# Attention's output projection on high and low parts, in a kernel of many sublayers

## The chip, the cores and the metric

The kernel runs on one core of one Trainium2 chip. The metric is the device time of one execution, in microseconds (us). The engines are named as in the profile: PE is TensorE (matmul), PEld its weight loads, ACT ScalarE, DVE VectorE, POOL GpSimd, SP SyncE. P is 128 partitions, T is 256 tokens, KT is 8 (1024 channels in tiles of 128).

## What is computed

A network of four blocks (each FFN, mixer, FFN, with modulated norms), followed by a second kind of block. The mixers are rwkv, mamba, attention, rwkv. The change is in the attention mixer: 16 query heads of 64, 4 key and value heads, a window of 128.

```
def swa_sink_attention(h, w_qkv, q_norm, k_norm, sinks, w_o):
    ...
    q, k, v = jnp.split(h @ w_qkv, [Hq * Dh, (Hq + Hk) * Dh], axis=-1)
    q = rms_norm(q...); k = rms_norm(k...)
    ...
        s = jnp.einsum('bqkgd,bskd->bkgqs', qb, kbb).astype(f32) * scale
        s = jnp.where(mb, s, NEG_INF)
        m = jnp.maximum(jnp.max(s, axis=-1, keepdims=True), sink)
        p = jnp.exp(s - m)
        denom = jnp.sum(p, axis=-1, keepdims=True) + jnp.exp(sink - m)
        return jnp.einsum('bkgqs,bskd->bqkgd', (p / denom).astype(vbb.dtype), vbb)
    ...
    return o @ w_o

x = x + gate[:, 1, None] * swa_sink_attention(adaln(x, ...), ...)
```

Each sublayer's shift, scale and gate come from `mod = silu(c) @ ada_w + ada_b`, a product of one vector with a large matrix that depends on no activation.

## The kernel before

Every engine has its own program, written out in order; semaphores join them. Weights stream from memory through SP into a ring of three slots of 24 blocks of 128x128 (L476, `weights`); a slot comes free when PE has taken the first block of the next (`Products.take`).

**Matmuls come in two kinds.** A plain one reads fp32 operands; it is recorded as two matmul records. One "on parts" replaces it by three matmuls on fp32r operands (`PAIRS`): weights high by values high, high by low, low by high. The high part is a copy by ACT (`Parts.high`, L1176, 128x1024 for eight blocks), the low part is the difference, taken by DVE (`Parts.low`, L1182). `w_part` is a ring of three such units. The queries and keys of attention are projected on parts (`parts.product`, 12 units); v, the scores, the transposes, the attended values and the output projection are plain.

**The loop over heads** in `sw_products` (PE), `sw_act` (ACT) and `sw_vector` (DVE) is a software pipeline of 19 steps n. In step n, PE makes `scores(n)`, `turns(n-2)` (transposes of the probabilities), half of an output projection tile (`outputs((n-5)//2, half)`, four of the eight output blocks that belong to the pair of heads t, L323) and `values(n-3)`. The projections accumulate in four PSUM banks that stay open for the entire loop. ACT makes the exponentials of head n, evicts the turned probabilities (`turned`), and in even steps evicts the values of a pair of heads (`out(t)`, L2952). DVE makes `largest(n)` (scale, mask and row maxima, L2992 to L2997) and `divided(n-1)` (L3002 to L3005).

**The modulation sums** fill DVE's gaps. `ada_sum` (L507) adds one chunk of 128x1536 of the modulation matrix, 16 chunks for each sublayer, here for the sublayer after next. The chunks come through POOL's queue into two buffers: `ada_stream` (L491) waits until chunk i has been summed, then issues chunk i+2 (768 KB). In attention, chunks 0 to 5 are summed between the projections, 6 to 12 in the odd steps 3 to 15 of the loop, and 13 to 15 behind it. Then DVE splits the first two weight units of the following FFN (`unit_low`, L885) and adds the mixer's output to x (`residual`, L845, eight tiles). ACT squares each new x tile, PE sums the squares (L323, 32 records with an output of 128x4), one small PE product spreads the reciprocal root, and the FFN starts (L928).

The lines at the heart of it:

```
    for n in range(17):
        if n < 16:
            largest(n)
        if n:
            divided(n - 1)
        ...
        elif n >= 3 and n % 2:
            ada_sum(k, dve, u + 2, len(SW_ADA) + (n - 3) // 2)
    for i in range(len(SW_ADA) + 7, ADA_STEPS):
        ada_sum(k, dve, u + 2, i)
```

## Time and profile before

| | us |
|---|---|
| median of 3 runs | 3070.55 (3070.54 to 3078.23) |
| the profiled execution, its own time | 3065.47 |
| its span | 3063.5 |
| PE busy | 2957.7 (97%) |
| DVE busy | 2368.5 (77%) |
| ACT busy | 1395.4 (46%) |
| mean granted TensorE clock | 0.982 |

The attention mixer's products start at 1565 us of the span, its loop over heads at 1612, and the FFN behind it at 1692. In the timeline views, each row is a start, a length, the engine, the line, what is written and read, a count of records, and in square brackets how long the engine was idle before it and what released it. Records of one engine overlap a little, so the step from one start to the next is the cost in a full queue, and the length is a little more.

### The profile page before, as it was taken

How to read it: one execution, taken by the hardware profiler on the slowest of the kernel's cores; microseconds unless marked ns; L12 is line 12 of the kernel's file. 1: busy time of each engine (PE TensorE's matmuls, PEld its weight loads, DVE VectorE, ACT ScalarE, POOL GpSimd, SP SyncE). 2: the span in 40 equal slices, each digit the busy share in tenths (PEclk: the TensorE clock that was granted, in tenths of full speed). 3: DMA queues.
4: the chain of work that ended last, by engine and by line, in shares of the span. 5: the costliest groups of instructions: out<-in, count | busy, mean ns of one | idle time of the engine just before them, and what ended most of it. 6: DMA issues, size and time to landing. Idle time of an engine off the chain costs nothing.

```text
span 3063.5 us, 50589 instructions
## 1 busy us (share of the span) xinstructions
PE 2957.7 (97%) x20226; PEld 2597.7 (85%) x20226; DVE 2368.5 (77%) x3515; ACT 1395.4 (46%) x2214; POOL 97.3 (3%) x187
## 2 busy tenths in 40 slices
PE   7999999999999999999999999999999999999998
PEld 6886788888888888888886888887788888989887
DVE  6988877998878857888867888887855866665685
ACT  4534023545545744545444554544123544465453
POOL 0000000000000000000000000000000000000000
PEclk9999999999999999999999999999999999999899
DMA  8783335686666227575764666672302553444453
GB/s 351 254 310 146 137 116 206 245 301 232 242 231 258 111 104 268 227 288 226 259 247 151 244 251 262 233 272 83 121 19 104 188 190 130 168 151 148 162 187 136
DMA packets 69674, 609.50 MB, mean 199 GB/s; under 512 B 7728, under 2 KB 7888, under 8 KB 31824
## 3 DMA queue, kind: packets, MB, share of 16 engines
q1 hardware_dynamic: 42768, 459.41, 40.3%
q0 software_dynamic: 26352, 144.85, 12.7%
q8 instruction: 161, 2.64, 0.3%
q10 hardware_dynamic: 336, 2.13, 0.2%
q14 instruction: 57, 0.47, 0.0%
HBM read 604.26 MB, written 2.10 MB: 198 GB/s over the span
## 4 chain that ended last, share of the span: by engine, by line
PE 84%; DVE 10%; ACT 3%; DMA 2%; issue 1%; SPq 0%; DVEq 0%; POOLq 0%; ACTq 0%
PE psum L325 25%; PE psum L928 23%; PE psum L932 12%; PE psum L949 10%; PE psum L956 6%; PE psum L323 4%; PE psum L953 1%; DVE arena L814 1%; PE psum L1726 1%; DVE ada_sum L507 1%; DMA weights<-in_weights 1%; DMA ada_in<-in_ada_w 1%; DVE arena L2366 1%; DVE unit_low L885 1%; DVE wkv_base L2102 1%
## 5 line engine op out<-in xcount | busy, mean ns | idle before, releaser
L879 ACT ACTIVATE unit_high<-weights 128x1024 fp32r<-128x1024 f32 x594 | 630.5, 1063 | 681.8 <-PE psum L932 389.5
L885 DVE TENSOR_TENSOR unit_low<-weights,unit_high 128x1024 fp32r<-128x1024 f32 x594 | 725.7, 1223 | 158.4 <-ACT unit_high L879 157.5
L928 PE MATMUL psum<-h_part,unit_high 128*128 128x512 f32 x3168 | 817.2, 395 | 21.2 <-DVE h_part L801 15.1
L928 PEld LDWEIGHTS psum<-h_part,unit_high 128*128 128x128 f32 x3168 | 574.2, 190 | 129.9 <-issue 17.4
L932 PEld LDWEIGHTS psum<-h_part,unit_low 128*128 128x128 f32 x3168 | 443.1, 191 | 29.5
L932 PE MATMUL psum<-h_part,unit_low 128*128 128x256 f32 x3168 | 464.7, 283 | 0.0
L325 PE MATMUL psum<-in_part,w_part 128*128 128x256 f32 x2784 | 358.6, 289 | 7.6 <-issue 3.2
L325 PEld LDWEIGHTS psum<-in_part,w_part 128*128 128x128 f32 x2784 | 344.9, 194 | 24.3 <-ACT arena L1214 11.3
L949 PE MATMUL psum<-hidden,unit_high 128*128 128x512 f32 x1386 | 350.0, 394 | 0.0
L1054 DVE TENSOR_REDUCE arena<-psum 128x256 f32<-128x512 f32 x396 | 272.9, 689 | 55.4 <-PE psum L932 44.5
L507 DVE SCALAR_TENSOR_TENSOR ada_sum<-ada_in,c_act,ada_sum 128x1536 f32<-128x1536 f32 x154 | 278.9, 1813 | 35.0 <-DMA ada_in<-in_ada_w 35.0
L949 PEld LDWEIGHTS psum<-hidden,unit_high 128*128 128x128 f32 x1386 | 249.9, 190 | 44.3
L325 PE MATMUL psum<-arena,weights 128*128 128x256 f32 (+4 forms) x1360 | 272.6, 372 | 6.1 <-DVE arena L1975 4.3
L325 PEld LDWEIGHTS psum<-arena,weights 128*128 128x128 f32 (+3 forms) x1360 | 216.1, 189 | 59.5 <-issue 28.2
L1182 DVE TENSOR_TENSOR w_part<-weights,w_part 128x1024 fp32r<-128x1024 f32 x144 | 175.2, 1221 | 89.1 <-ACT w_part L1176 88.4
L956 PEld LDWEIGHTS psum<-hidden,unit_low 128*128 128x128 f32 x1584 | 215.2, 191 | 13.4
L956 PE MATMUL psum<-hidden,unit_low 128*128 128x256 f32 x1584 | 221.6, 283 | 0.0
L325 PE MATMUL psum<-arena 64*64 64x64 f32 (+5 forms) x2752 | 184.1, 252 | 14.4 <-DVE arena L2083 6.9
L325 PEld LDWEIGHTS psum<-arena 64*64 64x64 f32 (+3 forms) x2752 | 151.6, 149 | 43.3 <-issue 16.4
L1176 ACT ACTIVATE w_part<-weights 128x1024 fp32r<-128x1024 f32 x144 | 151.0, 1051 | 16.5 <-PE psum L325 16.5
L491 POOL DMA_DIRECT2D ada_in<-in_ada_w x180 | 95.4, 530 | 1916.0 <-DVE ada_sum L507 1438.4
L1019 ACT ACTIVATE hidden<-arena 128x256 fp32r<-128x256 f32 x198 | 83.1, 420 | 86.9 <-DVE arena L1096 71.6
(315 smaller groups left out, 2721.1 us busy)
## 6 DMA issues: line engine op xcount, KB each, us to landing
weights<-in_weights SPq DMA_DIRECT2D x290, 1536.0 KB, 6.5
ada_in<-in_ada_w POOLq DMA_DIRECT2D x182, 768.0 KB, 6.1
consts<-in_consts POOLq DMA_DIRECT2D x1, 1668.0 KB, 16.2
x<-in_x SPq DMA_DIRECT2D x1, 1024.0 KB, 8.8
v_first<-arena ACTq DMA_DIRECT2D x1, 1024.0 KB, 4.9
arena<-v_first ACTq DMA_DIRECT2D x1, 1024.0 KB, 4.8
weights<-in_weights SPq DMA_DIRECT2D x1, 512.0 KB, 5.3
out<-x SPq DMA_DIRECT2D x1, 512.0 KB, 2.6
```

Source lines behind the costliest of these rows:

```text
L323: ins = self.k.nc.tensor.matmul(out, lhsT=w, rhs=x, start=start, stop=stop, skip_group_check=True)
L325: ins = self.k.nc.tensor.matmul(out, lhsT=w, rhs=x, start=start, stop=stop, is_transpose=turn)
L507: ins = k.nc.vector.scalar_tensor_tensor(out, buf, c, out, ALU.mult, ALU.add)
L879: k.nc.scalar.activation(k.unit_part[0][:, n % UNIT_RING], w, ACT.Copy).then_inc(k.sem["unit_high"], 1)
L885: k.nc.vector.tensor_tensor(k.unit_part[1][:, n % UNIT_RING], w, k.unit_part[0][:, n % UNIT_RING].bitcast(FP32), ALU.subtract).then_inc(k. ...
L928: mm(k.psum[:, 2 * (j % 2) + half, :].rearrange("p (i t) -> p i t", i=2), lhsT=part(2 * j + half, 0, t), rhs=k.h_parts[:, :, t], start=t = ...
L932: ins = mm(k.psum[:, 2 * (j % 2) + half, 0:T], lhsT=part(2 * j + half, 1, t), rhs=k.h_part[0][:, t], start=False, stop=t == KT - 1, skip_g ...
L949: mm(k.psum[:, out_bank(d), :].rearrange("p (i t) -> p i t", i=2), lhsT=w, rhs=x, start=f == 0, stop=f == FT - 1, skip_group_check=True)
L956: ins = mm(k.psum[:, out_bank(d), 0:T], lhsT=part(UNITS_UP + v, 1, b), rhs=k.hidden_part[f][:, 0], start=False, stop=f == FT - 1, skip_gro ...
L1054: v.tensor_reduce(to[:, j % RING], k.psum[:, 2 * (j % 2) + half, :].rearrange("p (i t) -> p t i", i=2), AX.X, ALU.add).then_inc(k.sem["gat ...
L1176: self.k.nc.scalar.activation(self.k.w_part[0][:, m % RING], w, ACT.Copy).then_inc(self.k.sem["w_high"], 1)
L1182: self.k.nc.vector.tensor_tensor(self.k.w_part[1][:, m % RING], self.weights(m)[1], self.k.w_part[0][:, m % RING].bitcast(FP32), ALU.subtr ...
```

## The change

The output projection goes onto parts. ACT's eviction of the attended values writes the high part, and DVE takes the low part straight from PSUM, in a new operation `out_low(t)` in front of `largest(n)` in odd steps. The bank of the values and the output tile are now released by DVE's operation (`sw_out_parted`) and not by ACT's. The eight units of output weights (one for each pair of heads) are split like the projection's: the first three in the last three turns of the projection, the others in even steps from 8 on by ACT and in odd steps from 9 on by DVE. The seven modulation chunks of the loop move from its odd steps 3 to 15 to its even steps 4 to 16. Behind the loop stand `out_low(6)`, the last unit's low part and `out_low(7)`, ahead of chunks 13 to 15. In the mamba mixer, a few semaphores are merged into one another, at the same places and events.

```
-    COUNTS = (48, 12, 84)
+    COUNTS = (48, 20, 84)
...
+SW_IN_UNITS = 12
+SW_BETWEEN = (12, 13)
+class SwParts(Parts):
+    def used(self, eng, m):
+        if m < SW_IN_UNITS:
+            super().used(eng, m)
+        else:
+            eng.wait_ge(self.k.sem["sw_unit_done"], m - SW_IN_UNITS + 1)
... (sw_products, PE)
     def values(i):
         pe.wait_ge(s["at_turned_read"], i + 1)
         if i % 2 == 0 and i:
-            pe.wait_ge(s["at_out_read"], i // 2)
+            pe.wait_ge(s["sw_out_parted"], i // 2)
...
     def outputs(t, half):
-        pe.wait_ge(s["at_out_read"], t + 1)
+        pe.wait_ge(s["sw_out_parted"], t + 1)
+        pe.wait_ge(s["w_parted"], parts.before + SW_IN_UNITS + t + 1)
         for d in range(4 * half, 4 * half + 4):
-            mm(out[:, d], pr.take(), z.o[:, t], t == 0 and d % 2 == 0, t == KT - 1,
-               s["mixed"] if t == KT - 1 and d % 2 else None, shared=True)
+            pr.take()
+            for i, (wp, xp) in enumerate(PAIRS):
+                end = s["mixed"] if t == KT - 1 and d % 2 else s["sw_unit_done"] if d == KT - 1 else None
+                mm(out[:, d], k.w_part[wp][:, (SW_IN_UNITS + t) % RING, d * P:(d + 1) * P], k.at_part[xp][t],
+                   t == 0 and d % 2 == 0 and i == 0, t == KT - 1 and i == 2, end if i == 2 else None, shared=True)
... (sw_act, ScalarE)
     def out(t):
         act.wait_ge(s["at_values"], 2 * t + 2)
-        act_(z.o[:, t], k.psum[:, 7, 0:T], f.Copy).then_inc(s["at_out_read"], 1)
+        act_(k.at_part[0][t], k.psum[:, 7, 0:T], f.Copy).then_inc(s["at_out_read"], 1)
...
         if n >= 3 and (n - 3) % 2:
             out((n - 3) // 2)
+        if n >= 8 and n % 2 == 0:
+            parts.high(act, SW_IN_UNITS + RING + (n - 8) // 2)
... (sw_vector, VectorE)
+    def out_low(t):
+        dve.wait_ge(s["at_out_read"], t + 1)
+        v.tensor_tensor(k.at_part[1][t], k.psum[:, 7, 0:T], k.at_part[0][t].bitcast(FP32), ALU.subtract)\
+            .then_inc(s["sw_out_parted"], 1)
     for n in range(17):
+        if n >= 5 and n % 2:
+            out_low((n - 5) // 2)
         if n < 16:
             largest(n)
...
-        elif n >= 3 and n % 2:
-            ada_sum(k, dve, u + 2, len(SW_ADA) + (n - 3) // 2)
+        elif n >= 4 and n % 2 == 0:
+            ada_sum(k, dve, u + 2, len(SW_ADA) + (n - 4) // 2)
+        if n >= 9 and n % 2:
+            parts.low(dve, SW_IN_UNITS + RING + (n - 9) // 2)
+    out_low(KT - 2)
+    parts.low(dve, SW_IN_UNITS + KT - 1)
+    out_low(KT - 1)
     for i in range(len(SW_ADA) + 7, ADA_STEPS):
         ada_sum(k, dve, u + 2, i)
```

DVE, the last full step of the loop with its neighbours, before (L2992 to L2997 are `largest`, L3002 to L3005 `divided`, L507 a modulation chunk):

```order
L3005 TENSOR_SCALAR arena<-arena,small 128x256
L507 SCALAR_TENSOR_TENSOR ada_sum<-ada_in,c_act,ada_sum 128x1536
L2992 SCALAR_TENSOR_TENSOR arena<-psum,consts 128x384
L2995 TENSOR_REDUCE small<-arena 128x1
L2996 TENSOR_REDUCE small<-arena 128x1
L2997 TENSOR_SCALAR small<-small,params 128x2
L3002 TENSOR_TENSOR small<-small 128x2
L3003 RECIPROCAL small<-small 128x2
L3004 TENSOR_SCALAR arena<-arena,small 128x128
L3005 TENSOR_SCALAR arena<-arena,small 128x256
L2992 SCALAR_TENSOR_TENSOR arena<-psum,consts 128x384
```

and now (`hidden<-psum,hidden` at L3028 is `out_low`, `w_part` at L1183 a weight unit's low part):

```order
L3024 TENSOR_SCALAR arena<-arena,small 128x256
L508 SCALAR_TENSOR_TENSOR ada_sum<-ada_in,c_act,ada_sum 128x1536
L3028 TENSOR_TENSOR hidden<-psum,hidden 128x256
L3011 SCALAR_TENSOR_TENSOR arena<-psum,consts 128x384
L3014 TENSOR_REDUCE small<-arena 128x1
L3015 TENSOR_REDUCE small<-arena 128x1
L3016 TENSOR_SCALAR small<-small,params 128x2
L3021 TENSOR_TENSOR small<-small 128x2
L3022 RECIPROCAL small<-small 128x2
L3023 TENSOR_SCALAR arena<-arena,small 128x128
L3024 TENSOR_SCALAR arena<-arena,small 128x256
L1183 TENSOR_TENSOR w_part<-weights,w_part 128x1024
```

The chunk that stood behind the divisions of an odd step is gone from there. An `out_low` stands ahead of that step and a weight split behind it, and the chunk comes a step later.

DVE, the end of the mixer, before (L845 is the residual):

```order
L507 SCALAR_TENSOR_TENSOR ada_sum<-ada_in,c_act,ada_sum 128x1536
L3002 TENSOR_TENSOR small<-small 128x2
L3003 RECIPROCAL small<-small 128x2
L3004 TENSOR_SCALAR arena<-arena,small 128x128
L3005 TENSOR_SCALAR arena<-arena,small 128x256
L507 SCALAR_TENSOR_TENSOR ada_sum<-ada_in,c_act,ada_sum 128x1536 x3
L885 TENSOR_TENSOR unit_low<-weights,unit_high 128x1024 x2
L845 SCALAR_TENSOR_TENSOR x<-psum,mod,x 128x256 x8
```

and now:

```order
L3024 TENSOR_SCALAR arena<-arena,small 128x256
L508 SCALAR_TENSOR_TENSOR ada_sum<-ada_in,c_act,ada_sum 128x1536
L3028 TENSOR_TENSOR hidden<-psum,hidden 128x256
L1183 TENSOR_TENSOR w_part<-weights,w_part 128x1024
L3028 TENSOR_TENSOR hidden<-psum,hidden 128x256
L508 SCALAR_TENSOR_TENSOR ada_sum<-ada_in,c_act,ada_sum 128x1536 x3
L886 TENSOR_TENSOR unit_low<-weights,unit_high 128x1024 x2
L846 SCALAR_TENSOR_TENSOR x<-psum,mod,x 128x256 x8
```

Two `out_low`, with a weight split between them, now stand between chunk 12 and the last three chunks.

PE, one step of the loop near its end, before (the L323 rows are `outputs`):

```order
L325 MATMUL psum<-consts,arena 128x128 x3
L323 MATMUL psum<-arena,weights 128x256 x4
L325 MATMUL psum<-arena 64x128 x3
L325 MATMUL psum<-arena 128x128
L325 MATMUL psum<-arena 128x256
L325 MATMUL psum<-consts,arena 128x128 x3
L323 MATMUL psum<-arena,weights 128x256 x4
```

and now:

```order
L325 MATMUL psum<-consts,arena 128x128 x3
L323 MATMUL psum<-hidden,w_part 128x256 x12
L325 MATMUL psum<-arena 64x128 x3
L325 MATMUL psum<-arena 128x128
L325 MATMUL psum<-arena 128x256
L325 MATMUL psum<-consts,arena 128x128 x3
L323 MATMUL psum<-hidden,w_part 128x256 x12
```

Four plain products have become twelve on parts; nothing else has moved.

## Rows read from the trace of the kernel before

**Rows 1.** The page: the span.

```profile
span 3063.5 us, 50589 instructions
```

**Rows 2.** Timeline of PE, one step of the loop: start, length, and so on.

```profile
1645.07 1.89 PE L323 MATMUL psum<-arena,weights 128*128 128x256 f32 x8
...
1648.55 0.55 PE L325 MATMUL psum<-consts,arena 128*128 128x128 f32 x3
1648.93 1.89 PE L323 MATMUL psum<-arena,weights 128*128 128x256 f32 x8
```

**Rows 3.** Timeline of DVE, part of the loop over heads.

```profile
1652.51 0.56 DVE L2992 SCALAR_TENSOR_TENSOR arena<-psum,consts 128x384 f32<-128x384 f32 x1 [1.45 <-PE psum L325]
...
1654.74 1.81 DVE L507 SCALAR_TENSOR_TENSOR ada_sum<-ada_in,c_act,ada_sum 128x1536 f32<-128x1536 f32 x1
```

**Rows 4.** Timeline of DVE, the end of the mixer.

```profile
1670.16 1.81 DVE L507 SCALAR_TENSOR_TENSOR ada_sum<-ada_in,c_act,ada_sum 128x1536 f32<-128x1536 f32 x1
...
1672.74 1.81 DVE L507 SCALAR_TENSOR_TENSOR ada_sum<-ada_in,c_act,ada_sum 128x1536 f32<-128x1536 f32 x1
1677.27 1.82 DVE L507 SCALAR_TENSOR_TENSOR ada_sum<-ada_in,c_act,ada_sum 128x1536 f32<-128x1536 f32 x1 [2.71 <-DMA ada_in<-in_ada_w]
1679.76 1.82 DVE L507 SCALAR_TENSOR_TENSOR ada_sum<-ada_in,c_act,ada_sum 128x1536 f32<-128x1536 f32 x1 [0.67 <-DMA ada_in<-in_ada_w]
1681.49 2.35 DVE L885 TENSOR_TENSOR unit_low<-weights,unit_high 128x1024 fp32r<-128x1024 f32 x2
1683.76 3.22 DVE L845 SCALAR_TENSOR_TENSOR x<-psum,mod,x 128x256 f32<-128x256 f32 x8
```

**Rows 5.** Timeline of POOL, two issues in that stretch.

```profile
1672.63 0.53 POOL L491 DMA_DIRECT2D ada_in<-in_ada_w  x1 [7.18 <-DVE ada_sum L507]
1675.21 0.53 POOL L491 DMA_DIRECT2D ada_in<-in_ada_w  x1 [2.05 <-DVE ada_sum L507]
```

**Rows 6.** Timeline of PE, the end of the mixer and the norm.

```profile
1679.03 0.87 PE L325 MATMUL psum<-arena 128*64 128x128 f32 x6
1680.37 3.72 PE L323 MATMUL psum<-arena,weights 128*128 128x256 f32 x16 [0.47 <-ACT arena L2952]
1684.83 3.71 PE L323 MATMUL psum<-consts,arena 128*128 128x4 f32 x32 [0.74 <-ACT arena L693]
1688.47 0.86 PE L325 MATMUL psum<-ada_sum,consts 128*32 128x128 f32 x24
...
1690.21 1.51 PE L325 MATMUL psum<-ada_sum,consts 128*32 128x128 f32 x24
```

**Rows 7.** Timeline of PE: products on parts in the projection.

```profile
1585.96 11.77 PE L325 MATMUL psum<-in_part,w_part 128*128 128x256 f32 x96
```

**Rows 8.** Timeline of DVE at a weight split; by form, a product from PSUM.

```profile
1596.27 1.22 DVE L1182 TENSOR_TENSOR w_part<-weights,w_part 128x1024 fp32r<-128x1024 f32 x1 [1.66 <-ACT w_part L1176]
1597.41 3.54 DVE L507 SCALAR_TENSOR_TENSOR ada_sum<-ada_in,c_act,ada_sum 128x1536 f32<-128x1536 f32 x2
...
L2983 DVE SCALAR_TENSOR_TENSOR arena<-arena,params,psum 128x256 f32<-128x256 f32 x12 | 5.1, 476 | 1.5 <-PE psum L325 1.5
```

**Rows 9.** Timeline of PE: norm sums ahead of the last FFN.

```profile
2855.76 6.99 PE L323 MATMUL psum<-consts,arena 128*128 128x4 f32 x32 [2.21 <-ACT arena L693]
```

**Rows 10.** Busy time and clock by stretch: the norms of both places.

```profile
core 0: us, PE busy (x) PEld busy (x) DVE busy (x) ACT busy (x) POOL busy (x), PEclk, DMA share, GB/s
1686.00:1688.00 2.00, 2.00 (x20) 2.00 (x19) 0.98 (x3) 1.43 (x4) 0.00 (x0) 1.00 0.90 347
1690.00:1691.00 1.00, 1.00 (x18) 0.75 (x20) 0.91 (x3) 0.17 (x1) 0.00 (x0) 0.50 1.07 455
...
2856.00:2858.00 2.00, 2.00 (x11) 2.00 (x11) 2.00 (x6) 1.25 (x3) 0.00 (x0) 0.50 0.00 0
```

**Rows 11.** Timelines of POOL and DVE: a chunk issued, its sum.

```profile
1536.14 0.53 POOL L491 DMA_DIRECT2D ada_in<-in_ada_w  x1 [5.06 <-DVE ada_sum L507]
...
1543.93 1.82 DVE L507 SCALAR_TENSOR_TENSOR ada_sum<-ada_in,c_act,ada_sum 128x1536 f32<-128x1536 f32 x1 [1.80 <-DMA ada_in<-in_ada_w]
```

More of the change, by code:

```diff
@@ L397, in layout @@
                      for j in range(FT)]
+    k.at_part = [[hidden_high[:, 4 + t // 2, t % 2] for t in range(KT)], [hidden_low[:, 1 + t // 2, t % 2] for t in range(KT)]]
     k.h_part = [k.h_parts[:, i] for i in range(2)]
@@ L449, in layout @@
               "wk_var", "wk_deviation", "wk_gn", "wk_out_turned", "wk_out_read",
-              "mb_silu", "mb_dt_abs", "mb_dt_exp", "mb_acum", "mb_cols", "mb_cols_read", "mb_x_turned",
+              "mb_silu", "mb_dt", "mb_acum", "mb_cols", "mb_x_turned",
               "mb_x_read", "mb_b_read", "mb_cb", "mb_masked", "mb_seg_sum", "mb_bounded", "mb_exp",
               "mb_mt", "mb_y", "mb_y_read", "mb_state_read", "mb_gated", "mb_squares", "mb_group_sum",
-              "mb_rms", "mb_rstd", "mb_spread", "mb_normed",
+              "mb_root", "mb_spread", "mb_normed",
               "at_scored", "at_added", "at_max", "at_exp", "at_prob", "at_turned", "at_turned_read",
               "at_values", "at_out_read", "sw_squares", "sw_head_sum", "sw_rstd", "sw_spread",
-              "sw_rms", "sw_normed",
+              "sw_rms", "sw_normed", "sw_out_parted", "sw_unit_done",
               "b2_rotated", "b2_rotated_read", "b2_rope", "b2_gate", "b2_gate_read", "b2_open", "b2_lam", "b2_angle",
@@ L2442, in opening @@
         else:
-            pe.wait_ge(s["mb_cols_read"], 1)
+            pe.wait_ge(s["mb_cols"], 2)
         for b in range(2):
@@ L2471, in first_chunk @@
         if g == 5:
-            pe.wait_ge(s["mb_rms"], 1)
+            pe.wait_ge(s["mb_root"], 1)
         pe.wait_ge(s["mb_x_read"], g + 1)
@@ L2497, in spread @@
     def spread(pair, bank):
-        pe.wait_ge(s["mb_rstd"], pair // 2 + 1)
+        pe.wait_ge(s["mb_root"], 2 * (pair // 2) + 2)
         for n in range(2):
@@ L2608, in root @@
         act_(z.rms, k.psum[:, 7, T:2 * T], f.Sqrt, bias=k.const("eps"), scale=1.0 / 256)\
-            .then_inc(s["mb_rms"], 1)
+            .then_inc(s["mb_root"], 1)
     part = 0
@@ L2620, in mb_act @@
             act_(z.neg_a, k.param("mb_A_log", rows=32), f.Exp)
-            act.wait_ge(s["mb_dt_abs"], 1)
-            act_(z.e32, z.e32, f.Exp, scale=-1.0).then_inc(s["mb_dt_exp"], 1)
+            act.wait_ge(s["mb_dt"], 1)
+            act_(z.e32, z.e32, f.Exp, scale=-1.0).then_inc(s["mb_dt"], 1)
         elif m == 14:
@@ L2627, in mb_act @@
             act_(z.acum_cols, cols[:, 1], f.Copy)
-            act_(z.cols[:, 1], cols[:, 1], f.Copy, scale=-1.0).then_inc(s["mb_cols_read"], 1)
+            act_(z.cols[:, 1], cols[:, 1], f.Copy, scale=-1.0).then_inc(s["mb_cols"], 1)
     for g in range(G):
@@ L2714, in inverse @@
     def inverse(half):
-        dve.wait_ge(s["mb_rms"], half + 1)
-        v.reciprocal(z.rms, z.rms).then_inc(s["mb_rstd"], 1)
+        dve.wait_ge(s["mb_root"], 2 * half + 1)
+        v.reciprocal(z.rms, z.rms).then_inc(s["mb_root"], 1)
     def normed(pair, bank):
@@ L2730, in mb_vector @@
             dve.wait_ge(s["evacuated"], q0 + MB_PLAIN + 1)
-            v.scalar_tensor_tensor(z.e32, z.dtx, -1.0, z.dtx, mult, ALU.max).then_inc(s["mb_dt_abs"], 1)
+            v.scalar_tensor_tensor(z.e32, z.dtx, -1.0, z.dtx, mult, ALU.max).then_inc(s["mb_dt"], 1)
             continue
@@ L2735, in mb_vector @@
         if m == 6:
-            dve.wait_ge(s["mb_dt_exp"], 1)
+            dve.wait_ge(s["mb_dt"], 2)
             softplus_open(k, own, z.e32, z.z32, z.z32b)
@@ L2878, in outputs @@
     def outputs(t, half):
-        pe.wait_ge(s["at_out_read"], t + 1)
+        pe.wait_ge(s["sw_out_parted"], t + 1)
+        pe.wait_ge(s["w_parted"], parts.before + SW_IN_UNITS + t + 1)
         for d in range(4 * half, 4 * half + 4):
-            mm(out[:, d], pr.take(), z.o[:, t], t == 0 and d % 2 == 0, t == KT - 1,
-               s["mixed"] if t == KT - 1 and d % 2 else None, shared=True)
-    for m in range(parts.tiles):
+            pr.take()
[3 more added lines that the diff above has]
+                   t == 0 and d % 2 == 0 and i == 0, t == KT - 1 and i == 2, end if i == 2 else None, shared=True)
+    for m in range(SW_IN_UNITS):
         parts.product(pe, pr, m)
@@ L3591, in build @@
         sem = k.sem
-        parts = {kind: Parts(k, ("mamba", "attention").index(kind), slot, q, (MB_PLAIN,) if kind == "mamba" else ())
+        parts = {kind: (Parts if kind == "mamba" else SwParts)(k, ("mamba", "attention").index(kind), slot, q, (MB_PLAIN,) if kind == "mamba" else SW_BETWEEN)
                  for kind, _, slot, q, _ in subs if kind in ("mamba", "attention")}
```

## The prediction

> **What bounds the kernel now.** I read the page first: over the 3063.5 us of the span [rows 1] PE is the busy engine nearly everywhere, so the question is whether the attention mixer is one of the places where it is not. Then the timelines of PE and DVE over the loop over heads. In the steady steps PE is the bound. A step from one `outputs` to the next is 3.86 us without a gap: 1.83 for the four plain products of the output projection (1.89 long, less the 0.06 by which records overlap), 0.38 for the transposes (1648.55 to 1648.93), 0.80 for the values (0.87 long), and so 0.85 for the scores [rows 2, 6]. DVE goes round with it, two steps in 7.71 us, and waits 1.45 of them for scores [rows 3]. Within DVE's round a head (`largest` and `divided`) is 2.23 us from start to start, and a modulation chunk 1.73 (1679.76 to 1681.49) [rows 3, 4]. So 2 x 2.23 + 1.73 = 6.19 us of work stand in 7.71.
>
> The third view is the end of the mixer on DVE, PE and POOL. There, PE is not the bound. `values(15)` ends near 1679.8, the last eight output products end near 1684.0, but DVE works through chunks 13, 14 and 15, two FFN splits and only then the residual at 1683.76 [rows 4, 6]. The chunks obey their two buffers. Chunk 12 ends at 1671.89; POOL issues chunk 14 at 1672.63; DVE's wait for it ends at 1677.27, 4.64 later. Chunk 13 ends near 1674.47, chunk 15 is issued at 1675.21 and awaited until 1679.76, 4.55 later [rows 4, 5]. From the start of chunk 13 to the residual it is 11.02 us: 1.73 summed, 0.74 to the issue, 4.55 to land, 1.73 summed, 2.27 for the splits. Before, this chain ran beside the last steps of PE and ended about when PE did. The reader should see that chunk 13's start sets the residual, and that it started 1672.74, seven us before the values ended.
>
> **The change, part by part.** *PE.* Twelve products on parts replace four plain ones in each half. The projection's 96 records on parts take 11.77 us, 0.122 each, so a block of three is 0.366 [rows 7] against 1.83 / 4 = 0.457. Over 64 blocks PE needs 5.8 us less, and its step falls from 3.86 to 3.49.
>
> *DVE in the loop.* Two additions. A weight unit's low part is 1.14 us in a full queue (1596.27 to 1597.41) [rows 8]. `out_low` appears nowhere in the trace. It reads 128x256 from PSUM and SBUF; the nearest row is the product of the same size from PSUM, 0.476 long [rows 8], less the overlap of about 0.05 with the next: 0.43, bounds 0.35 and 0.50. From step 9 a round of two steps is 6.19 + 1.14 + 0.43 = 7.76 us of DVE work, all without a gap, against 7.71 before. DVE takes PE's place as the bound and the pace is unchanged. In steps 5 to 8 there is no weight split, but a closed chain through both engines: `out_low` 0.43, half a projection 1.46, values 0.80, scores 0.85, a head 2.23, the chunk that now stands ahead of the next `out_low` 1.73, handovers 0.2, together 7.7. So PE's 5.8 us vanish: I put DVE's first operation of step 15 where it was, at 1670.16 - 2.23 = 1667.93 [rows 4], plus 0.2 for the projection's last turn, where ACT's split of unit 14 precedes the squares that a PE sum awaits. Bounds: 2 earlier, if `out_low` and handovers come cheap, 2 later, if each round has 0.3 more.
>
> *ACT.* Five splits of about a microsecond in even steps and none of its waits is on the path: DVE's exponentials are a step ahead of their use. Without that cover each would cost its full length.
>
> *The end.* This is where the time goes. From 1667.93 DVE runs step 15's head 2.23, unit 18's low part 1.14, the last division 0.85 (chunk 12's end 1671.89 to chunk 13's start 1672.74 before [rows 4]), chunk 12 1.73, `out_low(6)` 0.43: 1674.3. Only now can PE start `outputs(6)`: 0.1 + 1.46 + values 0.80 + 1.46 + 0.80 = 1678.9. ACT evicts (0.5), `out_low(7)` follows (0.1 + 0.43), and chunk 13 begins at 1679.9. DVE has nothing to do between, because `out_low(7)`'s wait is queued ahead of chunk 13, whose data have long landed. Chunk 13 is 7.2 us later than before; the chain of 11.02 behind it stays, so the residual is 7.2 later, at 1690.9 (+0.2).
>
> *The transfer.* Chunk 15 is now issued at about 1682.4, while the 1.5 MB weight slot that PE's last projection tile frees near 1680 is still coming. Chunks issued alone landed in 4.55 and 4.64 us; one issued under a stream of weights was awaited 7.8 us (1536.14 to 1543.93) [rows 11]. One slot is not a stream: I add 1.0, bounds 0 and 3.2.
>
> *The clock.* PE ends the last products at 1680.0 + 2.9 = 1682.9 and gets its first norm sum about 1.07 us after the residual's start [rows 4, 6], near 1693: ten idle us where there were 0.74. The trace has the same 32 norm sums in both states. At a granted 1.00 they take 3.71 us [rows 6, 10]; behind an idle 2.21 us, at 0.50 (1.2 of 2.4 GHz), 6.99 [rows 9, 10]. They are on the path, so + 3.3. The batch of 24 modulation records behind them takes 0.86 warm and 1.51 cold [rows 6], + 0.65, and the small spread product after it about 0.25 more: + 0.9. Before, the clock was at 0.50 from 1690 too, shortly ahead of the FFN's first products [rows 10], so these begin cold in both cases; how much longer they now stay cold I take as 0.5, between 0 and 1.
>
> *Elsewhere.* Merged semaphores in mamba keep the same events: nothing. Each later sublayer begins behind this residual through the modulated norm, and PE is busy there, so nothing gives the delay back.
>
> **Sum.** 0.2 + 7.2 + 1.0 + 3.3 + 0.9 + 0.5 = + 13.1 us. The profiled execution took 3065.47 by its own time, 2.0 outside the span [rows 1], so the changed one's should be near 3078.6. The median of the runs is 5.1 above the profiled execution; on it the forecast is 3070.55 + 13.1 = 3083.6. A measurement tells 0.3%, 9.2 us, from no change.
>
> **The rivals.**
> (a) *The clock holds, or the transfer is undisturbed and the loop a little quicker.* With the tail alone, + 7.4 to + 9.1: 3078 to 3079.7, within 0.3%. For it: behind the 0.74 idle us of before it stood at 1.00 [rows 6, 10]. Against it: 2.21 idle us were followed by 0.50 [rows 9, 10], and here it is ten. Chance 0.12.
> (b) *The transfer of chunk 15 collides fully.* Weights and chunk together would take the 7.8 us of [rows 11]: + 2.2 over the forecast, 3085.8. For it: the FFN's slots are due just then. Against it: only one is free. Chance 0.15. The Trainium skill (DMA: Bandwidth & Descriptors, Issuing engines are not separate DMA queues) says that transfers issued from SP and GpSimd run on the same 16 engines and interleave, which speaks for this case.
> (c) *PE's saving gets through.* If `out_low` and the splits cost DVE next to nothing, PE would pace the loop and `values(15)` would end 5.8 earlier, at 1674.0; chunk 13 at 1675.0, 2.3 later than before, and the residual + 2.3, + 4.7 for the clock: 3077.6. Even this is not faster, since chunk 13 still waits for the last values. Chance 0.07. By the Trainium skill (FP8 and Floating Point Precision, TensorE Precision Notes) a true fp32 product is four passes, so three passes would be 0.343 of a microsecond by the plain block's time and PE's saving 7.3 us; the projection's rows say 0.366.
> (d) *Faster.* The residual must not be bound by the chunks. If chunk 13's wait were not in the way, it would run at 1674.7, its chain would end by 1685.7 and the loop's end by 1682; with a loop at PE's pace the norm would start up to 5.8 us earlier: 3065. It decides once chunk 13 starts before 1672.74. DVE's order in the program speaks against it. Chance 0.03.
> (e) *The loop itself gets slower*: rounds of 8.1 us, where a wait for `out_low` on PE and one for scores on DVE alternate; six rounds give + 2.3 more, 3086. Chance 0.10.
> The forecast has 0.53.
>
> **The numbers.** Slower by over 0.3% takes the forecast, (b), (e), less 0.01: 0.77. Within 0.3%: (a), (c) and some of a tail shorter than I have it: 0.20. Faster 0.03. The low end is that of (c) less a little, 3076.5, the high end (b) with (e), 3088; beyond them 2 in 10.
>
> **What would show it.** In the changed profile: `out_low(7)` on DVE behind an idle of 3 to 4 us, then chunk 13 near 1680; an idle of 3.5 to 5 us ahead of chunk 15; the norm sums 7 us long at a clock of 0.50; the projection's halves at 1.46 us; the first score operation of step 15 within 2 us of 1668. The prediction is wrong if DVE idles for scores in steps 9 to 15 (then PE or a wait is the bound), or if chunk 13 starts before `out_low(7)`.

## The result

| | us |
|---|---|
| before, median of 10 runs | 3070.7 (3066.68 to 3078.23) |
| changed, median of 10 runs | 3080.45 (3073.59 to 3087.32) |
| ratio | 1.0035, 95% interval 1.0025 to 1.0046 |
| changed, profiled execution, own time and span | 3079.77 and 3078.1 |

The changed kernel is slower, by 9.75 us between the medians and by 7.7 to 14.1 us by the interval. The two profiled executions lie 14.3 us apart (3079.77 and 3065.47), since that of before was 5.2 us under its median and that of the change 0.7 under its own.

### The loop over heads

The timeline of PE in the changed kernel, two steps:

```profile
1643.15 1.70 PE L323 MATMUL psum<-hidden,w_part 128*128 128x256 f32 x12 [0.44 <-DVE hidden L3028]
...
1646.42 0.55 PE L325 MATMUL psum<-consts,arena 128*128 128x128 f32 x3
1646.72 1.67 PE L323 MATMUL psum<-hidden,w_part 128*128 128x256 f32 x12
1648.32 1.72 PE L325 MATMUL psum<-arena 128*64 128x128 f32 x10
```

A half projection on parts is 1.60 us from start to start (1646.72 to 1648.32), where the plain one was 1.83 [rows 2]. The record that follows the transposes comes after 0.30, where it was 0.38. So a step of PE's own work fell from 3.86 to 3.55 us. But every second half now waits 0.44 us for `out_low` (L3028). The timeline of DVE, one round of two steps (`out_low`, score, split, score, chunk):

```profile
1648.76 1.81 DVE L508 SCALAR_TENSOR_TENSOR ada_sum<-ada_in,c_act,ada_sum 128x1536 f32<-128x1536 f32 x1
1650.49 0.42 DVE L3028 TENSOR_TENSOR hidden<-psum,hidden 128x256 fp32r<-128x256 f32 x1
1650.83 0.55 DVE L3011 SCALAR_TENSOR_TENSOR arena<-psum,consts 128x384 f32<-128x384 f32 x1
...
1653.05 1.22 DVE L1183 TENSOR_TENSOR w_part<-weights,w_part 128x1024 fp32r<-128x1024 f32 x1
1654.34 0.56 DVE L3011 SCALAR_TENSOR_TENSOR arena<-psum,consts 128x384 f32<-128x384 f32 x1
...
1656.57 1.81 DVE L508 SCALAR_TENSOR_TENSOR ada_sum<-ada_in,c_act,ada_sum 128x1536 f32<-128x1536 f32 x1
```

The round is 7.81 us (1648.76 to 1656.57), where it was 7.71. With a split in the round, DVE has lost its 1.45 idle us [rows 3] and waits only 0.15 us, ahead of 1654.34 (the split is 1.29 from start to start, where a full queue gives 1.14 [rows 8]). But the rounds of steps 5 to 8 are 7.81 as well. They have no split, and DVE still waits for scores in them, here in step 8:

```profile
1638.72 0.56 DVE L3011 SCALAR_TENSOR_TENSOR arena<-psum,consts 128x384 f32<-128x384 f32 x1 [1.21 <-PE psum L325]
```

So it is not DVE's work alone that sets the pace, but a closed chain through both engines: from the start of `out_low` (1650.49) to the half projection 0.47, that half 1.63, values and scores up to 1654.34 1.75, a head 2.23 and the chunk ahead of the next `out_low` 1.73, together 7.81.

From the first `largest` to the last it is 55.15 us (1611.29 to 1666.44), where it was 54.96 (1612.97 to 1667.93). PE's saving is gone.

### The end of the mixer

DVE, the rows that answer to [rows 4] (L508 the chunks, L886 the splits, L846 the residual):

```profile
1670.65 1.81 DVE L508 SCALAR_TENSOR_TENSOR ada_sum<-ada_in,c_act,ada_sum 128x1536 f32<-128x1536 f32 x1
...
1678.22 0.42 DVE L3028 TENSOR_TENSOR hidden<-psum,hidden 128x256 fp32r<-128x256 f32 x1 [3.82 <-ACT hidden L2969]
1678.57 3.54 DVE L508 SCALAR_TENSOR_TENSOR ada_sum<-ada_in,c_act,ada_sum 128x1536 f32<-128x1536 f32 x2
1687.87 1.82 DVE L508 SCALAR_TENSOR_TENSOR ada_sum<-ada_in,c_act,ada_sum 128x1536 f32<-128x1536 f32 x1 [5.76 <-DMA ada_in<-in_ada_w]
1689.60 2.35 DVE L886 TENSOR_TENSOR unit_low<-weights,unit_high 128x1024 fp32r<-128x1024 f32 x2
1691.87 3.22 DVE L846 SCALAR_TENSOR_TENSOR x<-psum,mod,x 128x256 f32<-128x256 f32 x8
```

`out_low(7)` stands behind an idle of 3.82 us, chunk 13 starts at 1678.57 behind it, and chunk 15 at 1687.87 behind 5.76 more. POOL, the rows that answer to [rows 5]:

```profile
1673.12 0.53 POOL L492 DMA_DIRECT2D ada_in<-in_ada_w  x1 [5.75 <-DVE ada_sum L508]
1681.03 0.53 POOL L492 DMA_DIRECT2D ada_in<-in_ada_w  x1 [7.38 <-DVE ada_sum L508]
```

Chunk 14 was issued at 1673.12 and had long landed. Chunk 15, issued at 1681.03, was awaited for 6.84 us, where it was 4.55 [rows 4, 5]. What the DMA engines moved meanwhile is in the queues' shares of two stretches of 2 us (q1 carries SP's weights, q0 POOL's chunks; packets, MB, share of 16 engines). From 1683 to 1685:

```profile
q1 hardware_dynamic: 66, 0.69, 80.8%
q0 software_dynamic: 18, 0.11, 13.2%
```

and from 1685 to 1687:

```profile
q0 software_dynamic: 156, 0.87, 103.6%
q1 hardware_dynamic: 7, 0.01, 1.6%
```

The weight slot that SP issued at 1679.26 held the engines until about 1685; the chunk got 13%, and everything afterwards. The Trainium skill (DMA: Bandwidth & Descriptors, Issuing engines are not separate DMA queues) says that both run on the same 16 engines and interleave. The trace agrees that they share them, at 80.8% to 13.2%.

PE, the rows that answer to [rows 6]:

```profile
1678.70 3.13 PE L323 MATMUL psum<-hidden,w_part 128*128 128x256 f32 x24 [0.93 <-DVE hidden L3028]
1692.94 6.96 PE L323 MATMUL psum<-consts,arena 128*128 128x4 f32 x32 [11.11 <-ACT arena L694]
1699.84 1.51 PE L325 MATMUL psum<-ada_sum,consts 128*32 128x128 f32 x24
...
1704.34 0.76 PE L929 MATMUL psum<-h_part,unit_high 128*128 128x512 f32 x1 [0.41 <-DVE h_part L802]
```

The last products end at 1681.8, then PE idles 11.11 us, the norm sums take 6.96 us and not 3.71, and the modulation batch 1.51 and not 0.86. The clock in the idle stretch:

```profile
core 0: us, PE busy (x) PEld busy (x) DVE busy (x) ACT busy (x) POOL busy (x), PEclk, DMA share, GB/s
...
1683.00:1684.00 1.00, 0.00 (x0) 0.00 (x0) 0.00 (x0) 0.00 (x0) 0.29 (x1) 1.00 0.95 406
1684.00:1685.00 1.00, 0.00 (x0) 0.00 (x0) 0.00 (x0) 0.00 (x0) 0.00 (x0) 0.77 0.93 393
1685.00:1686.00 1.00, 0.00 (x0) 0.00 (x0) 0.00 (x0) 0.00 (x0) 0.00 (x0) 0.50 1.06 442
```

PE's last product ended at 1681.8; the clock was at 1.00 until 1684, at 0.77 from 1684 to 1685, and at 0.50 (1.2 GHz) from there on, when the sums came.

### The profile page after: what moved, and what is told of

The parts are those of the page before. It is cut to its first block, busy times and chain, and to the rows that moved or that the text cites. A ratio compares the mean times of both kernels' runs of the same rounds, so it can differ in the third digit from the quotient of the medians.

```text
span 3078.1 us, 50761 instructions
## 1 busy us (share of the span) xinstructions
PE 2958.8 (96%) x20290; PEld 2603.7 (85%) x20290; DVE 2380.4 (77%) x3531; ACT 1399.9 (45%) x2222; POOL 97.3 (3%) x187
## 4 chain that ended last, share of the span: by engine, by line
PE 84%; DVE 10%; ACT 3%; DMA 2%; issue 2%; SPq 0%; DVEq 0%; POOLq 0%; ACTq 0%
PE psum L325 24%; PE psum L929 24%; PE psum L933 12%; PE psum L950 10%; PE psum L957 6%; PE psum L323 3%; PE psum L954 2%; DMA weights<-in_weights 1%; DVE ada_sum L508 1%; PE psum L1727 1%; DVE arena L815 1%; DVE arena L2367 1%; DMA ada_in<-in_ada_w 1%; DVE wkv_base L2103 1%; DVE small L2102 1%
## 5 line engine op out<-in xcount | busy, mean ns | idle before, releaser
L886 DVE TENSOR_TENSOR unit_low<-weights,unit_high 128x1024 fp32r<-128x1024 f32 x594 | 725.8, 1223 | 161.2 <-ACT unit_high L880 160.4
L508 DVE SCALAR_TENSOR_TENSOR ada_sum<-ada_in,c_act,ada_sum 128x1536 f32<-128x1536 f32 x154 | 278.9, 1813 | 34.4 <-DMA ada_in<-in_ada_w 34.0
L1183 DVE TENSOR_TENSOR w_part<-weights,w_part 128x1024 fp32r<-128x1024 f32 x152 | 185.0, 1221 | 93.2 <-ACT w_part L1177 92.5
L1177 ACT ACTIVATE w_part<-weights 128x1024 fp32r<-128x1024 f32 x152 | 159.3, 1050 | 17.2 <-PE psum L325 15.9
```

The costliest lines, as they stand in the source:

```text
L508: ins = k.nc.vector.scalar_tensor_tensor(out, buf, c, out, ALU.mult, ALU.add)
L886: k.nc.vector.tensor_tensor(k.unit_part[1][:, n % UNIT_RING], w, k.unit_part[0][:, n % UNIT_RING].bitcast(FP32), ALU.subtract).then_inc(k. ...
L1177: self.k.nc.scalar.activation(self.k.w_part[0][:, m % RING], w, ACT.Copy).then_inc(self.k.sem["w_high"], 1)
L1183: self.k.nc.vector.tensor_tensor(self.k.w_part[1][:, m % RING], self.weights(m)[1], self.k.w_part[0][:, m % RING].bitcast(FP32), ALU.subtr ...
```

## The experiments

A profiled execution shifts as a whole by a few microseconds from run to run, so the local times below are counted from the loop's first `largest` (the first record of 128x384 on DVE). "FFN" is the first product of the following FFN. Ratios are to before, run on the same chip, with 95% intervals; before's medians beside the experiments were 3067.4 to 3068.1, so kernels of different rows are compared by their ratios. One execution of each kernel was profiled, and it can lie far from its kernel's median: e3's 6.3 us under it, e8's 5.1 under, e9's 7.9 over.

| kernel | last `largest` | chunk 13 | residual | norm sums take | FFN | median us | ratio |
|---|---|---|---|---|---|---|---|
| before | 54.96 | 59.77 | 70.79 | 3.71 | 79.15 | 3070.7 | |
| changed | 55.15 | 67.28 | 80.58 | 6.96 | 93.05 | 3080.45 | 1.0035 (1.0025 to 1.0046) |
| e1 wait alone | 54.96 | 67.37 | 80.75 | 6.96 | 93.22 | 3079.91 | 1.0044 (1.0032 to 1.0056) |
| e2 chunk 13 first | 55.15 | 63.03 | 74.31 | 6.96 | 86.78 | 3073.94 | 1.0017 (1.0008 to 1.0027) |
| e3 PE kept busy | 55.17 | 67.28 | 80.52 | 5.46 | 91.49 | 3078.25 | 1.0036 (1.0022 to 1.0049) |
| e4 a product less | 54.89 | 66.05 | 79.26 | 6.96 | 91.73 | 3077.43 | 1.0037 (1.0022 to 1.0052) |
| e5 no splits in the loop | 52.76 | 63.26 | 76.56 | 6.96 | 89.04 | 3074.93 | 1.0024 (1.0011 to 1.0038) |
| e6 chunks moved alone | 53.35 | 59.44 | 70.61 | 6.46 | 82.59 | 3069.17 | 0.9996 (0.9984 to 1.0009) |
| e7 end reordered | 57.51 | 65.40 | 71.46 | 4.42 | 81.71 | 3066.03 | 1.0002 (0.9989 to 1.0015) |
| e8 e7, splits in even steps | 54.30 | 62.18 | 68.24 | 3.81 | 77.88 | 3066.41 | 0.9993 (0.9978 to 1.0009) |
| e9 e8, norm kept busy | 54.29 | 62.17 | 68.23 | | 81.64 | 3066.72 | 0.9997 (0.9988 to 1.0006) |
| e10 before, end reordered | 56.23 | 61.04 | 69.83 | 3.63 | 79.26 | 3065.01 | 0.9989 (0.9979 to 0.9999) |

**e1: the wait alone, on the kernel before.**

```
+    dve.wait_ge(s["at_out_read"], KT)
     for i in range(len(SW_ADA) + 7, ADA_STEPS):
         ada_sum(k, dve, u + 2, i)
```

> The kernel before with one wait more and nothing else: DVE waits for ACT's eviction of the last pair of heads ahead of modulation chunks 13 to 15. My theory (the place of the chunks behind that wait is the loss): chunk 13 starts near 1680.4 of before's time and not at 1672.74, the residual 7.7 to 10 us later, norm sums 7 us long at a clock of 0.50, and the kernel 10 to 14 us slower than before, though nothing is on parts. Rival (the work added by the split, on DVE or ACT, is the loss): no change, within 2 us.

```profile
1681.46 3.55 DVE L507 SCALAR_TENSOR_TENSOR ada_sum<-ada_in,c_act,ada_sum 128x1536 f32<-128x1536 f32 x2 [7.52 <-ACT arena L2952]
1690.83 1.82 DVE L507 SCALAR_TENSOR_TENSOR ada_sum<-ada_in,c_act,ada_sum 128x1536 f32<-128x1536 f32 x1 [5.82 <-DMA ada_in<-in_ada_w]
```

DVE's timeline at the end is that of the changed kernel, with every product plain and no work added: chunk 13 7.6 us later than before, a wait of the same length for chunk 15, the sums at 6.96. The FFN starts 14.07 us late where the change made it 13.90. One wait in front of three chunks makes the loss by itself; the rival, the added work, falls.

**e2: chunk 13 ahead of the wait, on the changed kernel.**

```
     parts.low(dve, SW_IN_UNITS + KT - 1)
+    ada_sum(k, dve, u + 2, len(SW_ADA) + 7)
     out_low(KT - 1)
-    for i in range(len(SW_ADA) + 7, ADA_STEPS):
+    for i in range(len(SW_ADA) + 8, ADA_STEPS):
```

> The changed kernel with chunk 13 summed before the last low part of attended values, and chunks 14 and 15 behind it. My theory: chunk 13 fills DVE's idle 3.8 us, chunk 15 is issued near 1676.8 and not at 1681.0, before the weight slot that it met; it lands in 4.6 to 5.2 us, the residual is 4.5 to 6.3 us earlier, PE still idles over 4 us and the norm sums stay at 7 us; total 4 to 6 us less than the changed kernel. Rival (the chain of chunks is not what the residual waits for, the loop is): less than 1 us.

```profile
1676.47 1.81 DVE L508 SCALAR_TENSOR_TENSOR ada_sum<-ada_in,c_act,ada_sum 128x1536 f32<-128x1536 f32 x1
1680.37 0.42 DVE L3028 TENSOR_TENSOR hidden<-psum,hidden 128x256 fp32r<-128x256 f32 x1 [2.09 <-ACT hidden L2969]
...
1683.74 1.82 DVE L508 SCALAR_TENSOR_TENSOR ada_sum<-ada_in,c_act,ada_sum 128x1536 f32<-128x1536 f32 x1 [1.23 <-DMA ada_in<-in_ada_w]
...
1687.75 3.22 DVE L846 SCALAR_TENSOR_TENSOR x<-psum,mod,x 128x256 f32<-128x256 f32 x8
```

Chunk 13 fills the idle time, the residual is 6.27 us earlier after the loop's start (74.31 against 80.58), as much as the theory gave at most, and the ratio 1.0017, where it was 1.0035: 5.5 us of 3070. Chunk 15 was issued at 1678.93, ahead of the weight slot, and was awaited 4.81 us where it had been 6.84. PE still idled 4.84 us, and the sums stayed at 6.96.

**e3: PE kept busy up to the norm.** 88 matmuls that nobody reads, behind the last output product.

```
     outputs(KT - 1, 1)
+    for i in range(88):
+        k.nc.tensor.matmul(k.psum[:, 6, 0:T], lhsT=k.w_part[0][:, ..., 0:P], rhs=k.at_part[0][KT - 1], start=True, stop=True)
     pr.align()
```

> The changed kernel with 88 matmuls of 128x256 on PE behind the last output product, into a bank that nobody reads; they add nothing to the result. My theory: the residual starts where it did, the norm sums take 3.7 us at a clock of 1.00 and not 6.96, the batch of modulation products 0.86 and not 1.51, and the total is 3.5 to 4.3 us less than the changed kernel. Rival (the norm sums are long because of what waits or loads beside them, not the clock): unchanged, or longer by the matmuls.

PE's timeline, the added matmuls and the norm sums:

```profile
1683.56 10.72 PE L2941 MATMUL psum<-hidden,w_part 128*128 128x256 f32 x88
1694.75 5.46 PE L323 MATMUL psum<-consts,arena 128*128 128x4 f32 x32 [0.47 <-ACT arena L694]
```

and the clock in their stretches (PEclk is the third value from the end):

```profile
1683.50:1694.20 10.70, 10.70 (x90) 10.57 (x89) 5.01 (x6) 0.01 (x1) 1.05 (x2) 1.00 0.71 281
1694.80:1696.00 1.20, 1.20 (x12) 1.20 (x12) 1.20 (x4) 1.20 (x4) 0.00 (x0) 1.00 0.88 369
...
1697.00:1698.00 1.00, 1.00 (x7) 1.00 (x6) 0.00 (x0) 0.34 (x1) 0.00 (x0) 0.50 0.71 295
```

The residual is where it was. The clock held through the 88 matmuls and into the sums, then fell in their midst, though PE had no gap in them; the sums took 5.46 us, the modulation batch behind them 1.51 as before, and the FFN started 1.56 us earlier, where the theory had 3.5 to 4.3. So the clock does set the length of the sums, but idle time is not the only thing that lets it fall. The kernel before shows the same: PE has no gap from 1684.83 on [rows 6], the clock falls at the end of this row, and it is 0.50 behind it [rows 10].

```profile
1689.00:1690.00 1.00, 1.00 (x17) 0.78 (x8) 1.00 (x2) 0.00 (x0) 0.00 (x0) 0.76 1.00 424
```

The total does not tell e3 from the changed kernel (1.0036 and 1.0035).

**e6: the chunks moved to even steps, nothing else.**

```
-        elif n >= 3 and n % 2:
-            ada_sum(k, dve, u + 2, len(SW_ADA) + (n - 3) // 2)
+        elif n >= 4 and n % 2 == 0:
+            ada_sum(k, dve, u + 2, len(SW_ADA) + (n - 4) // 2)
```

> The kernel before with its seven chunks of the loop in the even steps 4 to 16 instead of the odd steps 3 to 15, nothing else. My theory: chunk 13 starts 1 to 1.5 us later than before and the residual with it, no long idle of PE, the norm sums warm, total + 0.5 to + 2 us. Rival (the later chunks are what costs): chunk 13 over 4 us later and 8 us or more in the total.

Not late at all: the chunks' old place at step 3 had cost the start of the loop 1.6 us, which came back (53.35 against 54.96), and the residual was 0.18 us earlier than before. PE was then done early, and idled. This is also the right neighbour for the changed kernel, which has its chunks in the same steps: against e6 its loop is 1.80 us longer (55.15 against 53.35). From step 4 to 6 it is 6.73 us here and 7.81 there, and further on 7.71 and 7.81 for two steps. So the parts did not leave the loop as it was, they made it longer, and the moved chunks hid that.

```profile
1687.07 6.46 PE L323 MATMUL psum<-consts,arena 128*128 128x4 f32 x32 [2.29 <-ACT arena L693]
...
1697.97 0.47 PE L928 MATMUL psum<-h_part,unit_high 128*128 128x512 f32 x1 [0.41 <-DVE h_part L801]
```

This is the cleanest price of the clock: the residual stands where it did, but behind an idle of 2.29 us (0.74 before) the sums are 6.46 us long, and the FFN starts 3.44 us late. The clock was still 1.00 when the sums began and fell within the first microsecond of them (0.80 from 1687 to 1688). In the median nothing of it is left (0.9996), and the profiled execution was 1.2 us over its median, so no total here shows what the clock costs. That the moved chunks are the loss is refuted.

**e4 and e5: who bounds the loop.** e4 leaves out the product of the weights' low part and the values' high part, so that part of the result is missing; all splits stay.

```
-            for i, (wp, xp) in enumerate(PAIRS):
+            for i, (wp, xp) in enumerate(PAIRS[:2]):
... (and `i == 1` for `i == 2` where a group ends)
```

> The changed kernel without the product of the weights' low part and the values' high part in the output projection, so this part of the result is left out; ACT's and DVE's splits stay. PE has 64 records of about 0.13 less, 8 us. My theory (DVE bounds the loop from step 9 on): the loop keeps 7.8 us for two steps there, PE only idles more, and the total is 1 to 2.5 us less, by the short products in the end alone. Rival (PE still bounds the loop): about 8 us less.

e5 also leaves out DVE's last five splits, whose low parts are then not read; PE waits for ACT's high part in their place, and later counts of `w_parted` are five lower.

```
-        pe.wait_ge(s["w_parted"], parts.before + SW_IN_UNITS + t + 1)
+        pe.wait_ge(s["w_high"], parts.before + SW_IN_UNITS + t + 1)
...
-        if n >= 9 and n % 2:
-            parts.low(dve, SW_IN_UNITS + RING + (n - 9) // 2)
...
-    parts.low(dve, SW_IN_UNITS + KT - 1)
```

> As the kernel with one product less, and in addition DVE's five weight splits of the loop and its end left out, since their low parts are no longer read (ACT's stay). My theory: DVE loses 1.14 us in each round of two steps from 9 on, and the loop falls to 6.9 to 7.4 us for two steps there, the start of the last chunks 1.5 to 4 us earlier than with one product less. Rival (the chain from the low part of values through PE back to DVE bounds it, and the splits are beside it): less than 1 us.

In e4, PE's half projection took 1.13 us and not 1.60; a round from step 9 on fell from 7.81 only to 7.65 (from 1644.41 to 1652.06 in its timeline). So PE was not the bound, but not quite out of it either: at 7.81 the bound is the closed chain, `out_low`, half a projection, values, scores, a head and a chunk; with a shorter projection, DVE's own work takes over at 7.65. The FFN started 1.32 us earlier than in the changed kernel, in the range of the theory, but the total is not less (1.0037 and 1.0035). In e5, the round was 7.33 throughout (1630.20 to 1637.53), the chain with the shorter projection, and chunk 13 came 2.79 us earlier than in e4. About 1.2 of that is a dip of the clock in e4's loop (one round of 8.84); the rest, 1.6, lies in the range expected. Both theories had a part of it: chain and DVE's own work are within 0.16 us of each other.

**e7: the end reordered.** On the changed kernel.

```
     parts.low(dve, SW_IN_UNITS + KT - 1)
+    ada_sum(k, dve, u + 2, len(SW_ADA) + 7)
+    for w in range(2):
+        unit_low(k, dve, ffn, w)
     out_low(KT - 1)
-    for i in range(len(SW_ADA) + 7, ADA_STEPS):
-        ada_sum(k, dve, u + 2, i)
+    ada_sum(k, dve, u + 2, len(SW_ADA) + 8)
... (ahead of the residual, the two `unit_low` only in mamba; behind it)
+                    if kind == "attention":
+                        ada_sum(k, dve, u + 2, ADA_STEPS - 1)
```

> The changed kernel with DVE's end written otherwise: chunk 13 and the two FFN splits ahead of the last low part of attended values, then chunk 14, the residual, and chunk 15 behind the residual. My theory: the residual starts 1.7 us behind the last low part, PE idles under 1 us and stays at a clock of 1.00, so both losses go: 10 to 13 us less than the changed kernel, and between 2 us faster and 1 us slower than before. Rival (a part of the loss sits in the loop or further on, or the modulation products now wait for chunk 15): more than 3 us of the loss stay.

```profile
1682.59 0.41 DVE L3028 TENSOR_TENSOR hidden<-psum,hidden 128x256 fp32r<-128x256 f32 x1
1682.92 1.81 DVE L508 SCALAR_TENSOR_TENSOR ada_sum<-ada_in,c_act,ada_sum 128x1536 f32<-128x1536 f32 x1
1684.65 3.22 DVE L846 SCALAR_TENSOR_TENSOR x<-psum,mod,x 128x256 f32<-128x256 f32 x8
```

The residual starts 2.06 us behind `out_low(7)`, and the ratio is 1.0002, where it was 1.0035: the loss is gone. In the profiled execution the loop was 2.4 us longer: PE idled 1.56 us at step 5, and the clock was at 0.50 from 1631 to 1637. PE then went from the last product to the norm sums without a gap, and yet the clock did not stay at 1.00, as the theory had it:

```profile
1686.04 4.42 PE L323 MATMUL psum<-consts,arena 128*128 128x4 f32 x32
```

and the clock, 0.84 in this row and 0.50 in the next:

```profile
1688.00:1689.00 1.00, 1.00 (x9) 1.00 (x10) 1.00 (x1) 0.32 (x1) 0.00 (x0) 0.84 1.02 430
```

**e8: the loop's order too.** On e7: chunks back to odd steps, DVE's splits in even ones.

```
-        elif n >= 4 and n % 2 == 0:
-            ada_sum(k, dve, u + 2, len(SW_ADA) + (n - 4) // 2)
-        if n >= 9 and n % 2:
-            parts.low(dve, SW_IN_UNITS + RING + (n - 9) // 2)
+        elif n >= 3 and n % 2:
+            ada_sum(k, dve, u + 2, len(SW_ADA) + (n - 3) // 2)
+        if n >= 10 and n % 2 == 0:
+            parts.low(dve, SW_IN_UNITS + RING + (n - 10) // 2)
```

> The kernel with the end reordered, and in its loop the modulation chunks back in the odd steps 3 to 15 and DVE's weight splits in even steps from 10 on. The changed kernel's round of two steps is 7.81 us and a closed chain: low part of values, half a projection, values and scores on PE, a head and then a chunk on DVE. My theory: with the split of 1.14 us in the chain instead of the chunk of 1.73, DVE's own work bounds the round, 7.6 to 7.7 us; the FFN starts 0.5 to 2 us earlier after the loop's first step than with the end reordered, and the total is 0 to 3 us less than before. Rival (DVE's own work is already the bound): no difference in the round.

```profile
1639.90 0.42 DVE L3028 TENSOR_TENSOR hidden<-psum,hidden 128x256 fp32r<-128x256 f32 x1 [0.66 <-ACT hidden L2969]
...
1662.46 0.42 DVE L3028 TENSOR_TENSOR hidden<-psum,hidden 128x256 fp32r<-128x256 f32 x1
```

Two different bounds show. The rounds without a split were 7.26 us, with DVE idle 0.66 of them ahead of `out_low` and no idle listed for PE: there PE, at 7.10 and the handovers, sets the pace, and its saving arrives. The rounds with a split were 7.65 (1659.10 to 1666.75), with no idle on DVE, as DVE's work alone gives. From the first `largest` to the last it is 0.66 us less than before (54.30 against 54.96), though the chunk is back in step 3. The FFN started 1.27 us earlier than before, and 3.83 earlier than in e7, which is outside the 0.5 to 2 expected because of the dip in e7's loop. In the median it cannot be told from before (0.9993).

**e9: matmuls between the norm sums**, on e8.

```
         norm_sum(k, pe, pr, n, t)
+        if n == 8:
+            for _ in range(2):
+                k.nc.tensor.matmul(k.psum[:, 6, 0:T], lhsT=k.w_part[0][:, 1, 0:P], rhs=k.at_part[0][KT - 1], start=True, stop=True)
```

> The same as the kernel with chunks in odd and splits in even steps, with two matmuls of 128x256 more on PE behind the records of each square tile in the norm ahead of the FFN; they go into a bank that nobody reads. My theory (the norm sums themselves let the clock fall, since they have 4 columns each): the clock stays at 1.00 through the sums, the 24 modulation records behind them take 0.86 us and not 1.51, and though the sums get 1 to 2 us longer by the 16 matmuls, the FFN starts within 1 us of the other. Rival (idle time alone lets it fall): the clock falls at the same place in the sums.

```profile
1695.00 0.50 PE L323 MATMUL psum<-consts,arena 128*128 128x4 f32 x4
...
1697.77 0.85 PE L323 MATMUL psum<-consts,arena 128*128 128x4 f32 x4
```

Four records of sums took 0.50 us up to 1696.2 and 0.85 from 1696.5 on, and the added pair went from 0.48 to 0.78: the clock fell in the midst of them all the same, the FFN started 3.76 us later than in e8. In e8 the clock had fallen too, only when the sums were nearly over:

```profile
1689.00:1690.00 1.00, 1.00 (x16) 0.95 (x19) 0.35 (x2) 0.26 (x1) 0.02 (x1) 0.54 1.04 428
```

The first sum was at 1685.77 there and at 1692.94 here, so the fall stands about as far behind it in both; the added matmuls did not move it, they made the sums long enough to run into it. My theory, that matmuls between the sums keep the clock up, is refuted in this form. What lets the clock fall here with PE busy stays open.

**e10: the kernel before with its end reordered** as in e7: chunk 13, the splits, chunk 14, the residual, chunk 15.

> The kernel before, all products of the output projection plain, with DVE's end reordered: chunk 13, the two FFN splits and chunk 14 behind the loop, then the residual, and chunk 15 behind it. My theory: the residual is bound by PE's last products and starts 1.5 to 2.5 us earlier than before, and the total is 1 to 2.5 us less than before. Rival (the last chunk is needed at once by PE's modulation products and gives the time back): within 0.5 us in the start of the FFN.

The residual came 0.96 us earlier, where 1.5 to 2.5 was expected, in spite of a dip of the clock that made the loop 1.27 us longer, and now waited for PE's products (1.56 idle us, released by PE). The FFN started at 79.26 against 79.15, within the 0.5 us of the rival; without the dip it would have been about 1.2 us earlier, so this profile does not decide between the two. At 0.9989 (0.9979 to 0.9999), a median of 3065.01 against 3067.41, it is the only kernel here whose interval lies under 1, and barely. It cannot be told from e8 either (0.9978 to 1.0009). So nothing here shows a gain from the parts, and of kernels that are equally fast by these runs this one is the simpler.

## Why the prediction was right

The direction, the place and the chain behind the last `out_low` were as forecast; the term of the loop came out near by luck, and the projection's end and the transfer were put too small. By its own steps, in the profiled executions: the terms below, from the end of the projection to the FFN, add up to 14.6 us, where the forecast had 13.1. That the two spans differ by 14.6 as well is chance. The changed execution was 2.4 us ahead when this stretch began (1595.26 against 1597.67) and lost 2.4 behind it.

- *The projection's end*: forecast + 0.2, measured + 0.73 (from the second PE head sum to the first `largest`, 16.03 against 15.30 us). The term was mis-sized because it left out DVE's queue. ACT's split of unit 13 waited until 1600.70 for its weight slot, so DVE's split at 1601.79, a chunk and another split stood ahead of the reciprocal that the loop waits for:

```profile
1601.79 1.22 DVE L1183 TENSOR_TENSOR w_part<-weights,w_part 128x1024 fp32r<-128x1024 f32 x1 [3.83 <-ACT w_part L1177]
1602.93 1.81 DVE L508 SCALAR_TENSOR_TENSOR ada_sum<-ada_in,c_act,ada_sum 128x1536 f32<-128x1536 f32 x1
1604.66 1.22 DVE L1183 TENSOR_TENSOR w_part<-weights,w_part 128x1024 fp32r<-128x1024 f32 x1
1605.80 1.75 DVE L2996 RECIPROCAL arena<-arena 128x256 f32<-128x256 f32 x1
```

- *The loop*: forecast no change, since DVE or the chain takes PE's place; measured + 0.19 in 55. That this came so near zero is partly luck: it is - 1.61 for the chunk that left step 3 (e6), a term that the prediction did not have, and + 1.80 for the parts. The prediction had the chain, at 7.7, as the bound of steps 5 to 8 and DVE's work, at 7.76, from step 9 on. The chain bounds both, at 7.81; DVE's work is 7.65 (e4, e8). PE saves 0.31 us in a step, 5.0 in all, and not 5.8: half a projection is 1.60 and not 1.46, and 0.08 less behind the transposes gives a part of that back. None of it reaches the time. What holds it back is the chunk between a head and `out_low`, which closes the chain. In e8, where the chunk stands elsewhere, the rounds are 7.26 without a split and 7.65 with one, so that DVE's work keeps the saving back only in the rounds with a split.
- *Chunk 13 behind `out_low(7)`*: forecast 7.2, measured 7.32 beyond the loop's 0.19. e1 makes the same delay with the wait alone, and e2 takes 6.3 of the residual's delay back by moving one chunk.
- *The transfer of chunk 15*: forecast + 1.0, measured + 2.28 (6.84 against 4.55). I had said that one slot is not a stream; it was enough to hold the chunk back until it had landed. On this term the full collision of rival (b), + 3.2, was nearer than the forecast, 0.9 off and not 1.3.
- *The clock*: sums + 3.3 forecast, + 3.25 measured; batch and spread + 0.9 and + 0.86. The FFN's first tile, forecast + 0.5, gave nothing (6.65 us to its second in both). In the changed kernel the clock fell while PE was idle, from 1.00 to 0.50 before a single sum had run. But the fall as such is not the change's doing: in all twelve profiles the clock fell to 0.50 somewhere in this norm or ahead of it, in the kernel before at 1689 to 1690, behind its last sum. What the change did was to bring it ahead of the sums. e3, e7 and e9 show that a PE kept busy would not have kept it through the norm.

Of the rivals, (a), (c) and (e) did not come: the clock fell, PE's saving did not get through, and the rounds were 7.81 and not 8.1. The condition of (d), chunk 13 not behind the last values, is what e8 makes: the norm sums begin 2.2 us earlier than before after the loop's start (69.63 against 71.86), where (d) had up to 5.8. On the median the change, 9.75, is less than the 13.1 forecast; the profiled execution of before stood 5.2 us under its median, and its local times carry no dip of the clock in the loop, while e4, e7 and e10 show dips of 1 to 2.5 us there. Whether such dips in other executions of before make up the difference was not measured.
